# Background projections in blocks of four contraction steps instead of one, in PE's queue of a three-layer transformer kernel

## The reference, cut to what matters

```python
# layer 1: gated linear attention in chunks, and chunked spatial gating
z = h @ w_in;  a_u, a_v, a_gate, b_q, b_k, b_v, b_gate, b_lr = split(z)
a_out = chunked_sgu(gelu(a_u), gelu(a_v), ...) * silu(a_gate)
o = gla_chunked(b_q, b_k, b_v, log_a);  b_out = rmsnorm(o) * silu(b_gate)
# layer 2: mLSTM in both directions (a recurrence over chunks) and attention in a window
qk = silu(centred_dwconv(qk, conv_w, conv_b))
h = mlstm_scan(q, k, v, ...) + flip(mlstm_scan(flip(q), flip(k), flip(v), ...))
# layer 3: gated delta rule in both directions, and attention over a 2-D neighbourhood
s = q_row @ k_band + bias;  p = softmax(where(in_window, s, -inf));  o = p @ v_band
```

## Time and profile before

| | us |
|---|---|
| median of 3 runs | 3860.85 (3857.14 to 3863.59) |
| the profiled execution | 3859.77 |
| its span | 3858.5 |
| PE busy | 3639.6 (94% of the span) |
| DVE busy | 2346.6 (61%) |
| ACT busy | 1653.5 (43%) |

### The profile page before, as it was taken

How to read it: one execution, slowest core, us unless ns; L and a number is a source line. 1 busy time by engine, 2 the same in 40 slices (tenths; PEclk the granted TensorE clock), 3 DMA queues, 4 the chain that set the end, 5 groups by cost and what they waited for, 6 DMA issues and landing times. The chain is left out here.

```text
span 3858.5 us, 54142 instructions
## 1 busy us (share of the span) xinstructions
PE 3639.6 (94%) x20112; PEld 2867.1 (74%) x20112; DVE 2346.6 (61%) x4124; ACT 1653.5 (43%) x3090; POOL 751.9 (19%) x555
## 2 busy tenths in 40 slices
PE   8999999998998887999999989999878888999998
PEld 5787788785766775888887857767667766888886
DVE  3344332325365757877768874666666658877777
ACT  4355222314455515333334374555433325556443
POOL 1000000373002214322210150111333421000013
PEclk9999999998998999999999999999989999999999
DMA  2100111582111112465546422111121105987662
GB/s 90 33 28 28 66 43 45 193 313 90 51 43 52 59 38 99 176 207 203 184 181 233 131 53 61 47 60 46 57 82 48 53 24 191 346 310 258 206 208 97
DMA packets 219493, 456.80 MB, mean 118 GB/s; under 512 B 30544, under 2 KB 44048, under 8 KB 219240
## 3 DMA queue, kind: packets, MB, share of 16 engines
q1 hardware_dynamic: 219240, 453.45, 34.5%
HBM read 334.28 MB, written 121.05 MB: 118 GB/s over the span
## 5 line engine op out<-in xcount | busy, mean ns | idle before, releaser
L1808 PE MATMUL b_ffn_space<-b_ffn_in_hi,b_ffn_wh 128*128 128x512 f32 x1932 | 756.0, 391 | 10.7 <-DVE b_ffn_in_x_low L1301 5.2
L1810 PE MATMUL b_ffn_space<-b_ffn_in_hi,b_ffn_wl 128*128 128x512 f32 x1932 | 752.7, 390 | 0.0
L1808 PEld LDWEIGHTS b_ffn_space<-b_ffn_in_hi,b_ffn_wh 128*128 128x128 f32 x1932 | 363.2, 188 | 95.5 <-issue 12.5
L1809 PE MATMUL b_ffn_space<-b_ffn_in_x_low,b_ffn_wh 128*128 128x512 f32 x1104 | 429.6, 389 | 0.0
L1810 PEld LDWEIGHTS b_ffn_space<-b_ffn_in_hi,b_ffn_wl 128*128 128x128 f32 x1932 | 363.2, 188 | 75.8
L1809 PE MATMUL b_ffn_space<-b_ffn_in_own_low,b_ffn_wh 128*128 128x512 f32 x828 | 323.2, 390 | 0.0
L1809 PEld LDWEIGHTS b_ffn_space<-b_ffn_in_x_low,b_ffn_wh 128*128 128x128 f32 x1104 | 207.2, 188 | 42.7 <-issue 0.2
L1867 ACT ACTIVATE b_ffn_wh<-b_ffn_raw 128x512 fp32r<-128x512 f32 (+1 forms) x188 | 112.7, 611 | 210.8 <-PE b_ffn_space L1810 209.5
L1809 PEld LDWEIGHTS b_ffn_space<-b_ffn_in_own_low,b_ffn_wh 128*128 128x128 f32 x828 | 156.0, 188 | 31.9
L1699 DVE TENSOR_TENSOR b_ffn_wl<-b_ffn_raw,b_ffn_wh 128x512 fp32r<-128x512 f32 x224 | 162.7, 727 | 17.0 <-ACT b_ffn_wh L1693 16.3
L1693 ACT ACTIVATE b_ffn_wh<-b_ffn_raw 128x512 fp32r<-128x512 f32 x224 | 134.8, 622 | 83.6 <-PE b_ffn_space L1810 83.5
(11 more groups left out here) (704 smaller groups left out, 8832.9 us busy)
## 6 DMA issues: line engine op xcount, KB each, us to landing
b_ffn_raw<-w SPq DMA_DIRECT2D x96, 256.0 KB, 4.2
b_ffn_raw<-w_ffn SPq DMA_DIRECT2D x44, 512.0 KB, 4.5
b_out_block<-w SPq DMA_DIRECT2D x40, 512.0 KB, 5.6
sums_ahead<-b_out_block SPq DMA_DIRECT2D x40, 512.0 KB, 4.3
b_ffn_raw<-sums_ahead SPq DMA_DIRECT2D x80, 256.0 KB, 4.2
b3f_y<-w SPq DMA_DIRECT2D x24, 512.0 KB, 6.3
b_ffn_sums<-b3f_y SPq DMA_DIRECT2D x24, 512.0 KB, 4.6
b_ffn_raw<-b_ffn_sums SPq DMA_DIRECT2D x48, 256.0 KB, 4.5
```

Of the source, the lines that this page charges most:

```text
L1808: self.nc.tensor.matmul(acc, self.weights.wh[w][:, wk], high[:, k], start=(k == 0), stop=False)
L1809: self.nc.tensor.matmul(acc, self.weights.wh[w][:, wk], low[:, k], start=False, stop=False)
L1810: last = self.nc.tensor.matmul(acc, self.weights.wl[w][:, wk], high[:, k], start=False, stop=(k == self.plan.rows(s) - 1))
```

## The change

The due time of a step is replaced by the mean due time of its block of four: steps 0 to 3 of a half are all due at the middle of their stretch, and so are steps 4 to 7. Equal due times keep the four together, twelve matmuls in a row. The waits inside `products` stay at their steps. Nothing else is changed, and no instruction is added or removed.

```diff
@@ class Feed
-    PIECE = DT // 2 * P
+    PIECE, TOGETHER = DT // 2 * P, 4
@@ def products(self, pe)
                 for k in range(DT):
-                    yield start + length * (half * DT + k) / (2 * DT)
+                    yield start + length * (half * DT + k // self.TOGETHER * self.TOGETHER + (self.TOGETHER - 1) / 2) / (2 * DT)
                     if half == 0 and k % (DT // 2) == 0:
                         pe.wait_ge(self.lo_done, 2 * b + k // (DT // 2) + 1)
```

## The result

| | before | after |
|---|---|---|
| median, us | 3858.99 (6 runs, 3853.0 to 3863.6) | 3887.73 (6 runs, 3883.7 to 3895.3) |
| ratio, 95% interval | | 1.0076 [1.0063, 1.0089] |
| the profiled execution | 3859.77 | 3883.72 |
| its span | 3858.5 | 3882.4 |
| PE busy | 3639.6 | 3639.4 |

The account below looks back on a forecast made before the run. PE was taken as the bound in four of five stages, with slack only in mlstm. Terms -5.5 + 4.6 + 5.2 + 2.9 + 7.2 + 2.8 + 0 = +17.2 us on 3859.77 gave 3877.0 us; range 3854 to 3896.

Parts of the forecast that it names:

- Passing with the whole array, 0: PE going between background and foreground matmuls on the whole array: no switch cost, so fewer runs gain 0 us.
- The rival that switches cost: Each switch costs PE about 0.09 us, so 159 fewer runs save 14 us: 3849 us, faster; chance 0.14.
- With part of the array, -5.5: Part-array runs in gqa and na: 29 new joins each remove two edges, 0.19 us, saving 5.5 us.
- its last rival: mlstm breaks down: DVE falls behind and slow half-speed stretches follow, mlstm terms 22 us, total 3897; chance 0.14.
- gqa, scores to transposes, +4.6: In gqa, 19 of 32 units lose covering steps between scores and transposes, so PE waits 4.6 us more.
- Transposes to products with nothing between, +5.2: In gqa and na, more units have no step covering ACT's copy: 2.8 and 2.4 us of waits.
- na, scores to transposes, +2.9: In na, 18 units lose one step of cover between scores and transposes, costing PE 2.9 us.
- the list of chains of na: The na chains given waits: scores to transposes and transposes to products; a norm's run counted only as cover.
- mlstm, +7.2: mlstm's recurrence: hops without a step rise from 14 to 42, 3.0 us, plus 4.2 us from DVE's normalisation.
- the ends, +2.8: Stage ends: fewer steps behind the last chain cost 1.4 us in mlstm and 0.7 each in gqa and na.
- The part of 4.2 us that was laid to DVE's normalisation pieces: In mlstm, DVE's normalisation between states delays the state by 0.3 us in half of 28 hops: 4.2 us.
- gla and sgu, 0: In gla, losses (+2.1) and gains (-2.0) of four units each cancel; sgu has hardly any idle PE: 0 us.

## Why the prediction was right, and where its sizes were off

The direction and the mechanism held: nothing is gained at the switches, and blocks take the cover from chains that PE waits for. The size was short by 11.5 us by the medians, and several terms were wrong in ways that partly cancel.

*Passing with the whole array, 0: right.* In sgu after the change sixteen instructions stand between two blocks:

```profile
501.72 0.39 PE L611 MATMUL sgu_feed_acc<-b_x_hi,sgu_feed_wl 128*128 128x512 f32 x1
501.94 1.95 PE L2566 MATMUL sgu_mix<-sgu_ws,all_x 128*128 128x128 f32 x16
503.64 0.48 PE L609 MATMUL sgu_feed_acc<-b_x_hi,sgu_feed_wh 128*128 128x512 f32 x1
503.96 0.40 PE L610 MATMUL sgu_feed_acc<-b_x_lo,sgu_feed_wh 128*128 128x512 f32 x1
```

From 501.72 to 503.96 are 2.24 us; less two background starts of 0.23 that is 1.78 for sixteen, 0.111 each, as for eight. The rival that switches cost is not borne out: 159 of 349 returns to the background are gone (counted in the traces), and blocks of two take 69 of them away without a gain (0.1% slower). In the two profiled executions mlstm's clock stayed at 0.90 and na's went from 0.99 to 0.98; over all profiles of either order the clock in mlstm was 0.89 to 0.91 before and 0.86 to 0.89 after, in na 0.98 to 0.99 and 0.97 to 0.98. The advice of the Trainium skill, Perfetto Trace Analysis, Matmul Optimizations, to issue matmuls back to back in batches because the engine scales its power with its use, lifted the clock of no stage here.

*With part of the array, -5.5: right as a rate.* Products, scores and six transposes in one run take 2.454 us in gqa after; apart they took 1.007 and 1.649 before, 0.20 more (by the distances between background starts around them, medians). The new order has 32 edges fewer in gqa, the 16 joins that were counted. Products and scores use different tilings, yet the join saved both edges: the rule of the Trainium skill, TensorEngine Tiling (Array Packing), Key Properties, by which a join would keep one drain, is not what this kernel shows. In gqa the gain shows: PE is busy for 237.5 to 237.9 us in four profiles of the new order against 239.8 to 240.0 in four of the old, 2.2 us less where 16 joins should give 3.0. In the profile of the changed kernel itself (239.7) and in na it does not show, and stretches at a lower clock are there to take it: behind a long wait the background matmuls of mlstm after start 0.57 and 0.43 us apart instead of 0.23,

```profile
1274.44 0.46 PE L3136 MATMUL mlstm_kv<-mlstm_vw,mlstm_kt 128*128 128x129 f32 x2 [3.22 <-DVE mlstm_state L3250]
...
1276.86 0.78 PE L609 MATMUL mlstm_feed_acc<-b2m_x_hi,mlstm_feed_wh 128*128 128x512 f32 x1
1277.43 0.63 PE L610 MATMUL mlstm_feed_acc<-b2m_x_lo,mlstm_feed_wh 128*128 128x512 f32 x1
1277.86 0.63 PE L611 MATMUL mlstm_feed_acc<-b2m_x_hi,mlstm_feed_wl 128*128 128x512 f32 x1
```

which is the 1.2 GHz level. In na 28 background matmuls of 1152 start over 0.35 us after the one before, against 13 before the change; at 0.22 us more each that is 3.3 us, which the forecast had in no term of its sum (only its last rival had such stretches), about what the joins of na (13 x 0.19 = 2.5) give. These counts differ between executions: 13 to 22 in four profiles of the old order, 28 to 41 in four of the new (19 in the one with the reciprocal sooner).

*gqa, scores to transposes, +4.6: right.* Its waits in the middle of the stage, one by one, were 0.4 us and are 5.1: +4.7.

*Transposes to products with nothing between, +5.2: too much.* The waits for the copies rose by 1.0 us in gqa (0.3 to 1.3) and 0.8 in na (0.4 to 1.2). Each wait was 0.3 to 0.4 us, not 0.7 and 0.8. The chain of 1.46 us was read to the end of both heads' copies; that the first head's products need only the first of them is the likely reason, which no run tested.

*na, scores to transposes, +2.9: did not come.* In the middle of the stage the waits were 6.0 us in five and are 5.3 in five. That units with twelve steps won back what others lost is likely, but was not followed unit by unit.

*The step that failed most: the list of chains of na had no head norms.* They were named in the front part as work that the change reorders, but used only as cover for others. Sums, root, reciprocal and spreading form a chain like the softmax's, and pay 6.3 us in the middle of the stage. Two experiments bear on it: with the reciprocal sooner 1.2 us of these waits went (1.8 less for the rows, 0.6 more for `na_done`), with the spreading later they moved. That the norms cost the stage their whole 6.3 us is therefore read from the waits, not shown by an edit that removes them. In the same way a copy of the queries by ACT in gqa and na, which the forecast had said could not get later by the change, now releases the first scores 0.8 us late in each: the projection's last steps stand directly before them.

*mlstm, +7.2, and the ends, +2.8: the size right, by luck in part.* The new order took 157.8 to 164.2 us in five profiles, the old one 150.8 to 153.6 in three, 8 us apart on average, where 8 to 9 were expected. But as waits only about half of it came: those for the state rose from 9.9 to 13.5 us, where about 17 was foreseen, and the idle time by 3.8. The other 4.4 us are busy time of PE. Some of it is in the bare hops, from one state product to the next with no background step between: they rose from 14 to 42, as counted, and one of eight instructions without a recorded wait took 0.92 to 0.99 us (medians of the five profiles) for 0.90 of work, so 28 of them come to 1 to 2.7 us. The rest is likely the lower clock (0.86 to 0.89 after 0.89 to 0.91). The part of 4.2 us that was laid to DVE's normalisation pieces stays open. In the profiles DVE is in them (L3273, L3278) for 5.8 of the 9.9 us that PE waited for the state before, and for 7.1 of the 13.5 after, which would be 1.3 us of the rise. The 3.22 us wait above falls where the second half of a head begins: DVE is in two such pieces until 1273.84, and ACT has the weights of that half ready only at 1273.51, so either alone would have held the step for most of it. The end's wait grew from 6.4 to 7.7 (1.4 foreseen), in gqa from 1.7 to 2.6, in na from 2.2 to 3.7: 3.7 us in all.

*gla and sgu, 0: right for sgu, wrong for gla.* The waits of gla rose from 4.0 us to 8.5 (transposes back 6.7, outputs for the state 1.4, scores 0.4), and the stage by 3 to 4 us (239.2 to 240.7 in six profiles against 235.0 to 236.6 in three). The losses of four units and the gains of four others did not cancel.

Together, by stage averages over the profiles of equal order: gla +3.6, sgu +0.4, gqa +5.9, mlstm +8.2, na +11.2, which is 29.3 us against 28.7 measured. Of these, 24.3 us are idle time, where the forecast had 22.7 of waits, and 5.0 are busy time, where it had 5.5 less. That the waits are so near is luck. The copies, na's scores to transposes and the waits for mlstm's state were put 3.4, 3.6 and 3.6 us too high, and the norms (6.3), gla (4.5) and the queries' copies (1.6) at nothing. So the sum as a whole missed mainly on the side of busy time: the joins were right as a rate, but PE was busy 4.4 us longer in mlstm and 2.4 in na, at a lower mean clock in both.

## What to carry to other kernels

When background work is regrouped, write down every chain that leaves the bound engine and comes back, norms and copies included, with its slack; each pays for itself, and the one left out of this list cost 6.3 us, which terms that were too large hid. Compare idle time and busy time of a stage apart: here the one repeated to about 2 us between executions and the other did not. Interleaving finely cost nothing on the whole array (0.111 us per instruction in runs of eight or sixteen), so fine grain was the safe choice here; only edges between whole-array and part-array matmuls had a price, 0.095 us, and placing the part-array ones next to each other saves it without large blocks. An edit that is to take work away has to be looked up in the trace: the pieces on 8 columns were as long as the full ones just where they mattered. Shifting one due time to cure a wait can move it to a chain with less slack: 6.9 to 3.0 us for one list of waits was paid with a new wait of 5.5.

## What the runs showed that was not expected

Grouping is not linear: two steps cost 0.1% (0.0 to 0.2 by the interval), four 0.76%, eight 2.86%. Equal code in one stage differed by 3 to 5 us between executions (na 465.4 to 470.4, gla 233.3 and 236.3), more than most single terms, while PE's idle time in na was 26.7 to 27.0 us in the same four profiles; so the waits one by one and several profiles were worth more than the time of a stage in one. And wider due times in gqa made PE about 3.2 us less busy with the same 1336 matmuls, most of it by fewer edges; whether those distances would help the old order too was not tried.
